# Attention weights of six heads turned by VectorE blocks and a trip through DRAM

## The reference

```python
def stick_breaking_attention(q, k, v):      # per block of 128 queries
    z = einsum('bhtd,bhsd->bhts', qb, kb) * scale
    causal = s_idx < t_idx
    log_beta = log_sigmoid(z)
    log_skip_j = where(causal, log_sigmoid(-z), 0.0)
    log_skip = cumsum(log_skip_j, axis=3, reverse=True) - log_skip_j
    weights = where(causal, exp(log_beta + log_skip), 0.0)
    out = einsum('bhts,bhsd->bhtd', weights, vb)

def stick_breaking_layer(h, norm_gain, w_in, q_gain, k_gain, w_out):
    u = rms_norm(h, norm_gain)
    q, k, v, gate = split(u @ w_in, 4)
    q, k = rms_norm(q, q_gain), rms_norm(k, k_gain)
    return (o * silu(gate)) @ w_out         # o: the heads' outputs, side by side
```

## Time and profile before

| | us |
|---|---|
| median of 3 runs | 1175.18 |
| lowest and highest | 1175.09, 1175.25 |
| span of the profiled execution | 1173.5 |
| TensorE busy | 1163.8 (99%) |
| VectorE busy | 796.7 (68%) |
| ScalarE busy | 419.7 (36%) |
| granted TensorE clock, mean | 1.000 |

### The profile page before, as it was taken

One profiled execution on the slowest core, in us unless ns is written; L12 is line 12 of the kernel. 1 busy time (PEld: TensorE's weight loads), 2 busy tenths in 40 slices (PEclk: granted clock), 3 DMA queues, 4 the chain that ended last, 5 costly groups with the idle time before them and its releaser, 6 DMA issues. The chain is left out here.

```text
span 1173.5 us, 20148 instructions
## 1 busy us (share of the span) xinstructions
PE 1163.8 (99%) x7228; PEld 1071.4 (91%) x7228; DVE 796.7 (68%) x1612; ACT 419.7 (36%) x911; POOL 149.8 (13%) x344
## 2 busy tenths in 40 slices
PE   8999999999999999999999999999999999999998
PEld 8999999999999999888888989898999999999787
DVE  5757485766767675774444778788888888788421
ACT  5535353545445454452222222323232322222200
POOL 2422121203031211110003100000000000000000
PEclk9999999999999999999999999999999999999999
DMA  8210223223142301066632110314142421117441
GB/s 251 57 53 19 73 82 112 68 83 103 67 119 73 109 1 46 1 228 218 209 108 73 55 36 20 115 66 137 70 145 72 133 86 45 45 37 296 148 139 72
DMA packets 110659, 113.51 MB, mean 97 GB/s; under 512 B 6880, under 2 KB 86752, under 8 KB 110560
## 3 DMA queue, kind: packets, MB, share of 16 engines
q1 hardware_dynamic: 110560, 112.23, 30.1%
HBM read 79.70 MB, written 32.51 MB: 96 GB/s over the span
## 5 line engine op out<-in xcount | busy, mean ns | idle before, releaser
L28 PE MATMUL p_proj<-w_qkv_hi,ut_hi 128*128 128x384 f32 x504 | 172.0, 341 | 0.2 <-DVE ut_lo L796 0.2
L30 PE MATMUL p_proj<-w_qkv_hi,ut_lo 128*128 128x384 f32 x504 | 169.1, 336 | 0.0
L29 PE MATMUL p_proj<-w_qkv_lo,ut_hi 128*128 128x384 f32 x504 | 168.7, 335 | 0.0
L28 PE MATMUL p_proj<-w_ig_hi,next_hi 128*128 128x256 f32 x512 | 145.5, 284 | 0.0
L29 PE MATMUL p_proj<-w_ig_lo,next_hi 128*128 128x256 f32 x512 | 143.1, 279 | 0.0
L30 PE MATMUL p_proj<-w_ig_hi,next_lo 128*128 128x256 f32 x512 | 143.0, 279 | 0.0
L28 PE MATMUL p_proj<-next_hi,w_qf_hi 128*128 128x512 f32 x282 | 113.2, 402 | 0.0
L30 PE MATMUL p_proj<-next_hi,w_qf_lo 128*128 128x512 f32 x282 | 110.1, 390 | 0.0
L29 PE MATMUL p_proj<-next_lo,w_qf_hi 128*128 128x512 f32 x282 | 109.8, 390 | 0.0
L808 DVE TENSOR_TENSOR_SCAN a_skip<-a_skip,a_diagonal 128x129 f32<-128x129 f32 (+3 forms) x64 | 86.9, 1358 | 30.2 <-ACT a_beta L648 28.4
L28 PEld LDWEIGHTS p_proj<-w_ig_hi,next_hi 128*128 128x128 f32 x512 | 96.2, 188 | 0.0
(11 more groups left out here) (255 smaller groups left out, 2732.3 us busy)
## 6 DMA issues: line engine op xcount, KB each, us to landing
stage<-in_hg_w_in_dram SPq DMA_DIRECT2D x32, 512.0 KB, 4.3
stage<-in_sb_w_in_dram SPq DMA_DIRECT2D x29, 512.0 KB, 5.9
w_out_hi_scratch<-m_in SPq DMA_DIRECT2D x32, 256.0 KB, 2.1
w_out_lo_scratch<-m_in SPq DMA_DIRECT2D x32, 256.0 KB, 2.3
m_in<-mixed_scratch SPq DMA_DIRECT2D x12, 448.0 KB, 6.1
a_beta<-in_x_dram SPq DMA_DIRECT2D x8, 512.0 KB, 4.3
m_in<-in_sb_w_out_dram SPq DMA_DIRECT2D x16, 256.0 KB, 3.6
ut_hi<-w_out_hi_scratch SPq DMA_DIRECT2D x8, 512.0 KB, 8.7
```

What stands on the lines that cost most here:

```text
L28: pe.matmul(out, w_hi, m_hi, start=start, stop=False, skip_group_check=True)
L29: pe.matmul(out, w_hi, m_lo, start=False, stop=False, skip_group_check=True)
L30: return pe.matmul(out, w_lo, m_hi, start=False, stop=stop, skip_group_check=True)
```

## The change

For heads 0 to 5 TensorE no longer turns the weights. VectorE turns each block of 32 x 32 within the weights of a tile and writes them to `skip` (`flip`). SP stores the tile to a scratch tensor in DRAM, `flips`. When that has landed, SP reads two quarters of the partitions back, and ScalarE issues the reads of the other two, in use i+1: each quarter of the partitions gets its runs of 32(j+1) columns from the four groups of 32 partitions. The reads land in the weights' own buffer; there are three such buffers now. ScalarE copies that to `wt_hi` in use i+2 ("settle") and VectorE makes `wt_lo`, one instruction each for a tile. `wt_hi` and `wt_lo` are laid out in quarters of 32 columns, and the outputs' matmuls read and write four runs of 32 for each block. The tables have a third place, "mid": ahead of the projection's wait for ScalarE and VectorE, and between the fourth and the fifth of its eight steps for TensorE. The outputs of pair g come at mid of use 4 + 2g, those of pair 3 at mid of the next head's use 0.

To make room for the third buffer, `k_scaled` and one `squares` are gone: GpSimd scales k in place, VectorE waits between its two sums of squares, and the first tiles of x are loaded to `gated`. ScalarE issues the loads of the weights from head 2 on. The halves of the output weights are split at uses 1, 2, 4 and 5. Heads 6 and 7 are turned by TensorE as before.

```diff
+    flips = nc.dram_tensor("flips_scratch", (TILES, P, SEQ), F32).ap()
...
     PLAIN = {"before": {i: [("scores", 0, i)] for i in range(TILES)},
-             "after": {i: ([("outputs", 0, (i - 3) // 2)] if i >= 3 and i % 2 == 1 else []) +
-                       ([("turn", 0, i - 1)] if 1 <= i <= TILES else []) for i in range(USES)}}
+             "mid": {i: ([("read", 0, i - 1)] if 1 <= i <= TILES else []) +
+                        ([("outputs", 0, i // 2 - 2)] if i >= 4 and i % 2 == 0 else []) +
+                        ([("settle", 0, i - 2)] if i >= 2 else [("outputs", -1, PAIRS - 1)] if i == 0 else [])
+                     for i in range(USES)},
+             "after": {}}
...
-    SPLIT_AT = [5, 6, 7, 9]
+    SPLIT_AT = [1, 2, 4, 5]
+    OUTPUTS_AT = KT // 2
+    SPLITS_AFTER = {1: ("store", 0), 2: ("load", 2), 3: ("store", 1), 4: ("load", 3), 5: ("store", 2), 6: ("store", 3)}
+    QUARTER = P // 4
+    CARRIED = HEADS - 2
...
+        def read_flipped(eng, h, j, c):
+            run = (j + 1) * QUARTER
+            eng.dma_start(flipped_blocks(h, j)[c * QUARTER:(c + 1) * QUARTER, :, :],
+                          flips[j, :, c * run:(c + 1) * run].rearrange("(g p) r -> p g r", g=4)
+                          ).then_inc(carried[j % 3], 16)
...
+            def carry(h, j, group):
+                sp.wait_ge(flipped, TILES * h + j + 1)
+                run = (j + 1) * QUARTER
+                sp.dma_start(flips[j, :, 0:4 * run], skip[j % 2][:, 0:4 * run]).then_inc(flip_stored[j % 2], 16)
+                sp.wait_ge(flip_stored[j % 2], 16 * (PAIRS * h + j // 2 + 1))
+                for c in range(2):
+                    if c == 1 and group is not None:
+                        for i in range(2):
+                            sp.wait_ge(link["w_parts_stored"][i], group * 64 + 64)
+                    read_flipped(sp, h, j, c)
...
-                        if i >= 2:
-                            act.wait_ge(weights_turned, UNITS * h + ENDS[i - 2])
-                        elif not known_first(h):
-                            act.wait_ge(weights_turned, UNITS * (h - 1) + ENDS[i + 6])
+                        if is_carried(h) or h == CARRIED and i < 2:
+                            if i >= 2 or not known_first(h):
+                                act.wait_ge(flip_stored[i % 2], 16 * (PAIRS * h + i // 2))
+                            if not is_carried(h):
+                                act.wait_ge(wt_ready, UNITS * (h - 1) + ENDS[6 + i])
+                            elif i >= 3:
+                                act.wait_ge(wt_ready, UNITS * h + ENDS[i - 3])
+                            elif not known_first(h):
+                                act.wait_ge(wt_ready, UNITS * (h - 1) + ENDS[(6, 7, 5)[i]])
...
+                    elif what == "read":
+                        act.wait_ge(flip_stored[tile % 2], 16 * (PAIRS * head + tile // 2 + 1))
+                        for quarter in range(2, 4):
+                            read_flipped(act, head, tile, quarter)
...
+            def settle_weights(h, j):
+                act.wait_ge(carried[j % 3], 64 * ((3, 3, 2)[j % 3] * h + j // 3 + 1))
+                if j >= 2 or not known_first(h):
+                    act.wait_ge(o_done, PAIRS * h + j // 2)
+                act.activation(slot_of(wt_hi, j), flipped_blocks(h, j), ACT.Copy).then_inc(wt_hi_ready, Z_UNITS[j])
...
+            def flip(h, i):
+                width = (i + 1) * P
+                dve.wait_ge(weights_ready, TILES * h + i + 1)
+                dve.transpose(skip[i % 2][:, 0:width].rearrange("p (c s i) -> p s c i", c=4, i=QUARTER),
+                              weights_of(h, i)[:, 0:width].rearrange("p (s c i) -> p s c i", c=4, i=QUARTER)
+                              ).then_inc(flipped, 1)
...
+            def refine_weights(h, j):
+                dve.wait_ge(wt_hi_ready, UNITS * h + ENDS[j])
+                dve.tensor_tensor(slot_of(wt_lo, j), flipped_blocks(h, j), slot_of(wt_hi, j).bitcast(F32),
+                                  ALU.subtract).then_inc(wt_ready, Z_UNITS[j])
...
+                    if plan is PLAIN and i == 5:
+                        load(h + 2, 3)
+                    if plan is PLAIN and i == USES - 1 and not (isinstance(h, int) and h == HEADS - 3):
+                        for p in range(3):
+                            load(h + 3, p)
...
+                            if kt == OUTPUTS_AT:
+                                attend(h, b, plan, "mid", i)
```

More of the change, by code:

```diff
@@ L63, in build_trunk, with link @@
         m_in = [sb(f"m_in{i}", [P, HEADS, P]) for i in range(2)]
-        def link(tag):
+        row_loaded = [ctx.enter_context(nc.semaphore(f"row_loaded{r}")) for r in range(HEADS)]
+        def link(tag, layer):
             def sem(name):
@@ L385, in build_attention @@
         raw = [sb(f"raw{i}", [P, 3, P]) for i in range(4)]
-        squares = [sb(f"squares{i}", [P, P]) for i in range(2)]
+        squares = sb("squares", [P, P])
         sum_sq = [sb(f"sum_sq{i}", [P, 2]) for i in range(2)]
@@ L440, in build_attention @@
         weights_ready = sem("weights_ready")
+        flipped = sem("flipped")
+        flip_stored = [sem(f"flip_stored{i}") for i in range(2)]
+        carried = [sem(f"carried{i}") for i in range(3)]
         weights_turned = sem("weights_turned")
@@ L469, in turn_events @@
             for i in range(USES):
-                for when in ("before", "after"):
+                for when in ("before", "mid", "after"):
                     if when == "after" and projects and i >= 3 and i % 2 == 1:
@@ L534, in load, with carry_all @@
                 load_columns(sp, stage, w_in, h, p).then_inc(w_loaded[p], 16)
+            def carry(h, j, group):
[8 more added lines that the diff above has]
+                    read_flipped(sp, h, j, c)
+            def carry_all(h, b, group, previous=None):
+                if group is not None:
+                    for i in range(2):
+                        load_raw_half(sp, m_in, w_out, link, group, i)
+                for j in range(TILES):
+                    carry(h, j, group if j == TILES - 1 else None)
+                    if j == 0 and previous is not None:
+                        store(previous, 1 - b)
+                    if group is not None and j in SPLITS_AFTER:
+                        what, part = SPLITS_AFTER[j]
+                        if what == "load":
+                            load_raw_half(sp, m_in, w_out, link, group, part)
+                        else:
+                            store_half(sp, m_in, w_out, link, group, part)
             def store(h, b):
@@ L570, in _ @@
                              allow_slow_non_contiguous=True).then_inc(small_loaded, 16)
[L571 to L575, removed]
+            carry_all(0, 0, None)
             with sp.Fori(0, 2) as pair:
                 for b in (1, 0):
[L578 to L581, removed]
+                    carry_all(pair * 2 + 2 - b, b, pair * 2 + 1 - b, pair * 2 + 1 - b)
+            carry_all(HEADS - 3, 1, None, HEADS - 4)
             store(HEADS - 3, 1)
@@ L822, in attend @@
                         weigh(head, tile)
+                        if plan is PLAIN:
+                            flip(head, tile)
+                    elif what == "settle":
+                        refine_weights(head, tile)
                     elif what == "outputs":
@@ L1083, in attend @@
             def attend(h, b, plan, when, i):
-                for what, d, tile in plan[when].get(i, []):
+                for what, d, tile in of_plan(plan, when, h, i):
                     head, half = of_head(h, b, d)
```

103 lines of the change are left out of this document (68 added, 35 removed).

## The result

The changed kernel took 1192.07 us (median of 4 runs, 1191.03 to 1193.41), the kernel before beside it 1175.22. The ratio is 1.0143 (95% interval 1.0128 to 1.0157): slower by 1.4%, 16.9 us. The forecast was slower, 1180.5 us; the measured time lies just over the upper end of its range, 1192. The profiled execution after, the fastest of its four, spans 1189.3 us, 15.8 more than the one before.

A forecast was written before the change was run, and what follows sets the result against it. TensorE, busy 99% of the span, was taken to bound the kernel. Sparing 23.8 us of turns against 28.8 to 29.4 us of stands gave +5 to +5.6 on 1175.18: 1180.5 us, range 1166 to 1192.

The forecast's parts named there:

- TensorE's turns: TensorE loses 216 weight turns in six heads at 0.11 us each, sparing 23.8 us, 3.96 a head.
- Products in runs of 32 columns: TensorE's products reading weights in runs of 32 columns cost 0, with 9.6 us over eight heads as upper bound.
- The ring: ScalarE's sigmoids and VectorE's chain alternate; tile 5's low part reaches TensorE 31.8 us after scores(4), TensorE arriving at 26.9.
- The stand: TensorE waits 4.9 us before pair 2's products for VectorE's low part, once in each of six heads.
- DMA at nothing: Transfers through DRAM and queue issues cost nothing: 3 us to spare, and 6 before VectorE would notice.
- each is wanted a use or more later: In SP's queue, head stores, raw halves and split halves stand between the turns; their delay was costed at nothing.
- The stand's effect on the clock: TensorE's work after each stand was priced at full speed, 0 us; only rival B gave it a cost.
- The sum: Spared 23.8 us against stands of 28.8 to 29.4: +5 to +5.6, added to the median 1175.18, giving 1180.5.
- Rival A: The ring stands as computed, without clock loss: 1180.5 us, own range 1177 to 1184; chance 0.45.
- B: As A, but each TensorE stand also costs 1.5 us by the lower clock, six times 9: 1189.5 us; chance 0.20.
- Rival C: The ring is shorter, so the change gains: 1165.8 us with half the stand, 1151.4 with none; chance 0.22.

The follow-up runs named there:

- that run: Kernel before, with TensorE turning only the last block of each unit in heads 0 to 5, 144 turns fewer: 1162.53 us, ratio 0.9887.
- a link doubled: Changed kernel with each of VectorE's block turns issued twice: 1222.81 us, ratio 1.0397 to the kernel before.
- the ask moved: Changed kernel with the products of pair 2 and settling of tile 6 put behind the first gate half: 1165.04 us, ratio 0.9912 to the kernel before.
- skip first: Changed kernel with ScalarE's `skip` sigmoids first, freeing the scan, and the buffer wait only ahead of `beta`: 1168.97 us, ratio 0.9947 to the kernel before.

## Where the prediction held, and the step that failed

**TensorE's turns, 23.8 us.** The measured price is 0.09 a turn for 144 of them, so 19.4 for 216. The 0.09 behind each of 48 groups (4.3) come on top; that run kept them, and they stand on a row only. Together 23.7: the term holds.

**Products in runs of 32 columns, 0.** They cost 0.36 us a block against 0.35: 0.01 for each of 160 blocks in eight heads, an estimated 1.6 us. This is inside the bound of 9.6.

**The ring, 31.8 us, and TensorE there at 26.9.** Right link by link; 31.5 and 27.2. One number in it does not come out of its rows: the products of pair 0 are 0.91 less three turns of 0.11, which is 0.58 and not 0.64, too little to matter. The stand was 4.3 where 4.9 was forecast, 25.8 us in six heads. Three runs show the mechanism: the sigmoids of `skip` taken out (23.1 us less), a link doubled (30.7 more), the ask moved (27.0 less).

**DMA at nothing.** Nearly right for the changed kernel: the carried tiles' stores landed in a median of 2.6 us, their reads in 2.3. Not seen was that the load of the fourth output half would wait in SP's queue: ScalarE stood 6.3 us for it in four heads, in front of the sigmoids of tile 6. In the head shown this cost nothing, for these sigmoids started at 297.71 and the low part of tile 3, which they need too, was only there at 297.60. With SP's reads doubled it decided. The sentence "each is wanted a use or more later" was too easy.

**The stand's effect on the clock, at nothing: the step that failed.** The sum priced a stand at its own length, and put what follows it at full speed. Rival A (the stand alone, 0.45) was taken for likeliest, and B (the stand costs clock, 0.20) for a rival. B is what happened: the clock fell at each of six stands, and 23.7 us of work ran at 0.50. This term was 0 in the sum and is 11.1 us by the rows. Filling the stand with idle turns gave back 8.8 us by the medians, and 9.8 to 10.7 in the two runs without a fall. B's own price was 1.5 us a stand where the rows give 1.9; its time, 1189.5, is 2.6 under the result. The rule of the Trainium skill ("TensorE: Matmul & The Clock Gate", Part 1) that an idle array falls to the lower clock until it has been busy again is borne out by the rows: in the head shown the clock was at 0.50 through the 5.80 us of work behind the stand, and at 1.00 from 320.3 to 381.5. Against it I had put only that no row of before showed a stand; that is no evidence that a stand is free.

**The sum.** -23.7 + 25.8 + 1.6 + 11.1 is 14.8, and the profiled executions differ by 15.8; one microsecond is not assigned. The medians differ by 16.9; the other 1.1 is the distance of the profiled execution from its median. One head agrees: 63.5 before, less 3.96, with 0.2 for the products, 4.3 of stand and 1.6 of clock is 65.6, and the two heads between 195.13 and 260.93 and between 327.93 and 393.75 took 65.8 from one scores(0) to the next.

**Rival C** (a shorter ring makes it faster) is wrong for this kernel and right as advice: the ring without the sigmoids of `skip` gives 1168.97, and with the low part ahead of the turn 1158.71.

## What to carry to other kernels

When a buffer's release is made by the last engine of a pipeline and waited for by the first, add up one turn of the ring from the trace's rows and hold it against the bottleneck's time for that step; busy shares of 70% and 35% show nothing of it. Put the wait ahead of the one instruction that needs the buffer, not ahead of its group, and put the instruction that frees it ahead of those that do not. A stand of TensorE of 4.3 us cost 1.9 us more by the clock in this kernel, and stands of 1.4 us none: look in a trace for what stands of the length at hand do to the granted clock before pricing them at their length alone. If the stand can't be removed, idle turns in it gave back most of that.

## What the runs showed of the hardware

Gaps of 4.5 to 4.8 us between matmul starts came each with a stretch at 0.50 of 3.41 or 6.83 us; it began between 1.6 us ahead of the first product and 0.3 behind it. In the run with doubled turns one came behind a gap of 2.2 us between starts (the rows from 99.40), while in the run with skip first two gaps of 1.9 us and one of 2.7 left the clock at 1.00. Length of the stand alone does not tell which. 36 turns of the 128 x 128 identity in 4.09 us were followed by products at the higher level, in five of six heads; in the sixth a wait of 3.0 us came behind them. Block turns of VectorE cost 0.18 us and 1.04 ns a column, in 128 x 256 as in 128 x 1024:

```profile
L925 DVE STREAM_TRANSPOSE a_skip<-a_beta 128x1024 f32<-128x1024 f32 x6 | 7.5, 1245 | 0.2
...
L925 DVE STREAM_TRANSPOSE a_skip<-a_beta 128x256 f32<-128x256 f32 x6 | 2.7, 445 | 0.2
```
